# The modulation matmuls: one 512-column block per pair of ring slots in place of four blocks side by side in each slot

## What is computed

```python
silu_c, silu_cc = jax.nn.silu(c), jax.nn.silu(c_ctx)
for l in range(DEPTH_2):                                  # 2 layers
    mod = (silu_c @ w_mod[l] + b_mod[l])[:, None, :]
    mod_c = (silu_cc @ w_mod[l] + b_mod[l])[None, None, :]
    sh_m, sc_m, gt_m, sh_f, sc_f, gt_f = jnp.split(mod, 6, axis=-1)
    ...
    h = modulate(x, g_pre_mix[l], sh_m, sc_m)
    ...                                                   # attention, FFN, gates
```

## Time and profile before

| | |
|---|---|
| median of 3 runs | 1714.01 us (1713.75 to 1714.54) |
| the profiled execution | 1714.01 us, its span 1712.2 us |
| mean granted TensorE clock | 0.945 of full |
| TensorE busy | 1579.7 us (92%) |
| VectorE / ScalarE / GpSimd busy | 713.1 / 577.5 / 542.8 us |
| w_mod loads | 96 DMAs of 512 KB |

### The profile page before, as it was taken

The page is one execution under the profiler, slowest core; times in us unless marked ns, Lnnn a source line. Parts: engine busy times, 40 slices in busy tenths (PEclk is TensorE's granted clock), DMA queues, the critical chain, the costliest instruction groups (busy, mean ns, idle before and its releaser), DMA issues. The chain is left out here.

```text
span 1712.2 us, 18498 instructions
## 1 busy us (share of the span) xinstructions
PE 1579.7 (92%) x6550; PEld 1073.9 (63%) x6550; DVE 713.1 (42%) x1473; ACT 577.5 (34%) x784; POOL 542.8 (32%) x167
## 2 busy tenths in 40 slices
PE   6998899986999998999999999999999899699996
PEld 4774455442777755465467777777774465287775
DVE  4767633025233243633357333563225443442323
ACT  3442243012444320144034433344331353243432
POOL 3556100001555520000024555555540000055553
PEclk9999855997999999899999999999999999799998
DMA  6535232337555534455345555555454322845541
GB/s 214 177 103 198 74 123 99 123 121 272 172 172 180 168 108 150 144 174 196 116 155 172 171 172 172 173 172 174 172 180 132 117 92 86 284 153 172 171 172 49
DMA packets 164348, 266.47 MB, mean 156 GB/s; under 512 B 13364, under 2 KB 106680, under 8 KB 164152
## 3 DMA queue, kind: packets, MB, share of 16 engines
q1 hardware_dynamic: 161992, 263.35, 46.7%
q10 hardware_dynamic: 2288, 2.23, 0.4%
HBM read 264.50 MB, written 1.05 MB: 155 GB/s over the span
## 5 line engine op out<-in xcount | busy, mean ns | idle before, releaser
L1234 POOL TENSOR_TENSOR w_l<-ring,w_h 128x1024 fp32r<-128x1024 f32 x148 | 495.5, 3348 | 1125.6 <-ACT w_h L934 1125.6
L934 ACT ACTIVATE w_h<-ring 128x2048 fp32r<-128x2048 f32 x148 | 283.0, 1912 | 292.1 <-PE G L522 289.1
L1465 DVE TENSOR_TENSOR w_l<-ring,w_h 128x1024 fp32r<-128x1024 f32 x148 | 196.6, 1328 | 366.5 <-ACT w_h L934 366.3
L520 PE MATMUL G<-w_h,xT_h 128*128 128x512 f32 x704 | 288.4, 410 | 21.3 <-DVE bd L1478 7.4
L521 PE MATMUL G<-w_l,xT_h 128*128 128x512 f32 x704 | 279.6, 397 | 0.0
L522 PE MATMUL G<-w_h,xT_l 128*128 128x512 f32 x704 | 279.1, 397 | 0.0
L501 PE MATMUL G<-ring,HT 128*128 128x512 f32 (+2 forms) x544 | 219.6, 565 | 3.2 <-issue 1.7
L520 PEld LDWEIGHTS G<-w_h,xT_h 128*128 128x128 f32 x704 | 133.7, 190 | 67.2 <-issue 19.6
L501 PEld LDWEIGHTS G<-ring,HT 128*128 128x128 f32 x544 | 101.0, 191 | 118.1 <-issue 115.6
L522 PEld LDWEIGHTS G<-w_h,xT_l 128*128 128x128 f32 x704 | 133.3, 189 | 32.8
L521 PEld LDWEIGHTS G<-w_l,xT_h 128*128 128x128 f32 x704 | 133.5, 190 | 28.2 <-issue 0.2
(11 more groups left out here) (245 smaller groups left out, 1710.8 us busy)
## 6 DMA issues: line engine op xcount, KB each, us to landing
ring<-in_w_ffn_in SPq DMA_DIRECT2D x132, 512.0 KB, 4.7
ring<-in_w_mod SPq DMA_DIRECT2D x96, 512.0 KB, 4.6
ring<-in_w_ffn_out SPq DMA_DIRECT2D x66, 512.0 KB, 4.2
ring<-in_w_in SPq DMA_DIRECT2D x48, 512.0 KB, 4.6
ring<-in_w_ffn_gate SPq DMA_DIRECT2D x22, 512.0 KB, 3.8
ring<-in_w_ffn_up SPq DMA_DIRECT2D x22, 512.0 KB, 4.8
ring<-in_w_ffn_down SPq DMA_DIRECT2D x22, 512.0 KB, 4.3
ring<-in_we_in SPq DMA_DIRECT2D x16, 512.0 KB, 4.6
```

The source lines that it names most:

```text
L520: nc.tensor.matmul(dst, a, w_h, start=start, stop=False)
L934: nc.scalar.activation(split_h[n % 2], ring1[:, s % RING, :], ACT.Copy).then_inc(w_hi, 1)
L1234: nc.gpsimd.tensor_tensor(split_l[b][:, half], ring1[:, (first + i) % RING, half], split_h[b][:, half].bitcast(F32), ALU.subtract).then_in ...
L1465: V.tensor_tensor(split_l[n % 2][:, half], ring1[:, s % RING, half], split_h[n % 2][:, half].bitcast(F32), ALU.subtract).then_inc(w_lo_dve, 1)
```

## The change

The same groups in the same ring slots with as many DMAs and matmuls, but cut the other way. Slots 2q and 2q+1 of a group now hold column block q: the first with input chunks 0 to 3, the second with chunks 4 to 7. They are loaded with `half_block`, so a run in DRAM is 512 columns (2 KB) where it was 1024 (4 KB). `mod_slot` now issues its four matmuls for one q and four chunks, and each q is summed over two slots.

```diff
             def mod_group(g):
-
                 s0 = prod[f"mod{g}"][0]
                 wv = chunks(w["w_mod_2"][g // 3])
                 for j in range(MODG):
-                    slot, c = (s0 + j) % RING, (g % 3) * 4 * NB
-                    fill(slot, s0 + j, [(ring[:, slot, i * 2 * NB:(i + 1) * 2 * NB],
-                                         wv[:, j, c + i * 2 * NB:c + (i + 1) * 2 * NB]) for i in range(2)])
+                    c = ((g % 3) * 4 + j // 2) * NB
+                    half_block((s0 + j) % RING, s0 + j, wv, j % 2, slice(c, c + NB), NB)
...
             def mod_slot(g, j, bank):
-                s = prod[f"mod{g}"][0] + j
+                s, q = prod[f"mod{g}"][0] + j, j // 2
                 if g == 0 and j == 0:
                     pe.wait_ge(c_silu, 1)
                 landed(s)
-                for q in range(4):
-                    mm = nc.tensor.matmul(G[32 * q:32 * q + 32, bank, :], scT[:, j, :],
-                                          ring[:, s % RING, q * NB:(q + 1) * NB],
-                                          start=(j == 0), stop=(j == MODG - 1), tile_position=(0, 32 * q))
+                for k in range(4):
+                    mm = nc.tensor.matmul(G[32 * q:32 * q + 32, bank, :], scT[:, 4 * (j % 2) + k, :], ring4[:, s % RING, k, :],
+                                          start=(j % 2 == 0 and k == 0), stop=(j % 2 == 1 and k == 3),
+                                          tile_position=(0, 32 * q))
                 mm.then_inc(slot_read, 1)
```

## The result

The changed kernel takes 1773.8 us (median of 4, 1768.4 to 1776.8) for 1713.9 before, a ratio of 1.035 with a 95% interval of 1.033 to 1.037: slower by 60 us. The forecast was 1781, with 1766 to 1837 as its range. The profiled execution has a span of 1770.1 us for 1712.2, so 57.9 us are to be found in it.

What follows compares the result with a forecast made beforehand. TensorE, busy for 92% of the span, was taken as the bound. Terms a1 -13.1, ax +21.2, ac +20.7, a1x +20.7, mod1 +9.9, mod5 +7.4 sum to +66.8 on 1714.0: 1781 us, range 1766 to 1837.

Steps and rivals of the forecast that it cites:

- The slot, 3.59 us for 1.00: Attention slots at full clock: eight records follow one another at 0.433 us plus 0.13 edge, +2.59 us each.
- B: Rival: a tile's weight load can't hide behind the matmul on the same tile; +42 us, 1823 us; chance 0.10.
- D: Rival: a record costs less alone than in a batch, 0.25 to 0.40 us; 1753 us at 0.36; chance 0.08.
- E: Rival: a record takes 0.23 us, as fp32r ones in the FFN; -3 us, 1711 us; chance 0.03.
- The clock in a1: Stage a1: its first long slot brings back full clock, y_a then starts at full clock; -13.1 us in sum.
- rival A: One narrow tile doesn't bring a1's clock back from 1.2 GHz: +41.6 for -13.1, so 1836 us; chance 0.14.
- rival C: A narrow tile counts so little that the clock falls in mod1, mod5 and all attention: over 1970 us; chance 0.05.
- The loads at nothing: Weight DMAs of all groups: 2 KB runs in place of 4 KB cost 0 us.
- The cover that I called ample: Loads queued behind later slot reads: wanted three parts (21 us) after the last slot is read, against 4.6 us for landing.
- Less at most three records that can overlap where the tile changes: Lone group mod1: serial 27.7 us, at most three records overlapped gives 26.4; 27.1 taken, +9.9 us.
- The FFN behind mod1 at 0: FFN after mod1: its weights come earlier against the group's end, with no time priced for it.
- The transposes behind mod5, -2.2: Transposes after mod5 and of hf_x1, at half clock before, run at full clock: -2.2 us, within mod5's +7.4.

Runs made afterwards that it cites:

- one-tile kernel: Kernel before with its own 4 KB loads, but all four matmuls of every slot on column tile 0: 1782.0 us, ratio 1.0413.
- mod0 alone: The change made only for group mod0 in attention a1, all else as in the kernel before: 1698.6 us, ratio 0.9925.
- repeated slot: Kernel before with mod0's first slot issued four times (1680.8 us, ratio 0.9817) or twice (eight executions, 1677.1 to 1712.4 us).
- lone-groups kernel: The change made only for mod1 and mod5, attention as in the kernel before: 1722.1 us for 1710.9, ratio 1.0063.
- 0, 0, 1, 1: Kernel before with the four matmuls of a slot on column tiles 0, 0, 1 and 1 in that order: 1712.3 us.
- 0, 0, 0, 1: Kernel before with the first three matmuls of a slot on column tile 0 and the last on tile 1: 1743.2 us.

## Why the prediction was right, and where not

*The slot, 3.59 us for 1.00: right.* 3.55 measured, the loads of weights hidden. ax, ac and a1x together gave +61.2 for +62.6. Rivals B, D and E, which price the record otherwise, are out by the 0.431 us of the one-tile kernel. (The 2.9 us that rival D estimates for a slot doesn't come out of its own factor: 0.87 x 3.07 + 0.13 is 2.8.)

*The clock in a1: right, and the decisive term.* -10.8 and -2.8 for -10.2 and -2.9. That the first pair is so close is partly luck: the first slot took 4.81 us for the forecast 6.5, while attention took 34.6 us (59.4 less seven slots of 3.55) for the forecast 32.9, and the two misses of 1.7 us cancel. At rival A's half clock a1 would have cost +41.6 and the kernel 55 us more. The experiments with mod0 alone and with the repeated slot show the cause; rival C is out too, since mod1 stands at 1.00 on one narrow tile from 381.61 to 405.47. One sentence of the prediction was wrong, that no row shows a clock lost in attention once it was high: the trace of before has 1.00 from 217.0 to 218.4, when a1 has begun, and 0.50 from 220.0 on. It falls in a1's first two microseconds, after the 2.06 us in which TensorE stood idle ahead of it; that this gap is the cause was not tested.

By the Trainium skill ("TensorE: Matmul & The Clock Gate", Part 1, "What's actually happening") sustained activity releases the default half rate. The streams agree with it, and what the prediction called open is settled for this kernel: a stream on one tile of 32 columns brought the clock back in a1's first slot (4.81 us). But a busy engine wasn't enough: in a1 before TensorE is busy for 76.5 of 77.1 us and stays at half clock.

*The loads at nothing: right* for the run length (1712.1 for 1711.1). The cover that I called ample had one hole: at the third change of tile in mod1 the next weights weren't there, because the overlap lets that group run faster than I had reckoned (wanted at 397.1, landed at 398.5). It cost some 1.3 us, three records, by estimate from the 0.43 us of one.

*"Less at most three records that can overlap where the tile changes": the step that failed.* I let one record overlap at a change, where four do. mod1 came out at 23.9 us and not 27.1, mod5 with its eviction at 24.5 and not 27.9: 3.2 and 3.4 us less. Of the 8.9 us between forecast and trace this is most.

*The FFN behind mod1 at 0: missed by 2.7 us.* The prediction saw that the FFN's weights come earlier against the group's end and gave this no price. 1.4 us of it is this: ScalarE no longer waits for them, and TensorE's wait for VectorE's copy of x is 5.97 us for 7.37, which the lone-groups kernel shows as well. Part of the rest is the clock, back 4.2 us after the FFN's start (413.4 to 417.6) for 5.7 before (421.3 to 427.0).

*The transposes behind mod5, -2.2: the overlap failed.* They did run at full clock, but of the 2.2 us only 0.5 arrived. hf_x1's transposes and the FFN's first matmul, before and after:

```profile
1488.43 3.67 PE L588 MATMUL T<-ident,Y 128*128 128x128 f32 x16 [0.28 <-DVE modcol L1383]
1498.43 0.77 PE L520 MATMUL G<-w_h,xT_h 128*128 128x512 f32 x1 [6.33 <-DVE bd L1480]
```
```profile
1545.94 1.97 PE L586 MATMUL T<-ident,Y 128*128 128x128 f32 x16 [0.28 <-DVE modcol L1381]
1555.93 0.76 PE L518 MATMUL G<-w_h,xT_h 128*128 128x512 f32 x1 [8.03 <-DVE bd L1478]
```

From the start of the transposes to the FFN it is 10.00 us before and 9.99 after. The FFN waits for the chain on ScalarE and VectorE that starts with the modulation values (ScalarE's split of the weights, L934, waits 1.73 us for `hscale` before and 1.27 after), not for the end of the transposes, so what they saved (1.70 us) became wait.

## What to carry to other kernels

Matmuls with 32 columns of stationary operand cost about a quarter here when neighbours in the instruction stream go to different column tiles (a slot of 1.00 us for 3.55); a sum over chunks on one tile gives that up. Look at the granted clock of a stage before costing work in it: here added work made a stage shorter, and 4 us of thrown-away matmuls took 30 us off the kernel. Where a stage of small matmuls stands at half clock after an idle gap, a dense stream ahead of it is worth a try, but make it long enough to catch every time: 6 us caught in 5 executions of 5, 3.6 us in 4 of 8.

## What of the hardware I had not expected

TensorE starts a record for a free column tile past as many as three that wait for a busy one (0.00 us into the slot with 0, 0, 1, 1, 0.88 us with 0, 0, 0, 1), and across the border of two slots. And what clock a1 gets depends on the clock at its start: its mix of small matmuls and short slots stayed at 1.2 GHz for 76 us in the kernel before, where the clock fell in its first two microseconds, and at 2.4 GHz for 41.6 us where a stream had raised it first.
